# Tail of a hybrid decoder layer: SBUF regions placed at multiples of 256 bytes, and the output weights of the cross attention split two or three at a time

## The reference, cut to what matters

```
x = x + mixed @ w_out[l]
x = x + memory_cross_attention(rms_norm(x, ln_xattn[l]), mem_n, xa_wq[l], xa_wkv[l], xa_wo[l], xa_qn[l], xa_kn[l])
x = x + conv_glu_ffn(rms_norm(x, ln_ffn[l]), ffn_w_up[l], ffn_conv_w[l], ffn_conv_b[l], ffn_w_down[l])

def memory_cross_attention(h, mem_n, w_q, w_kv, w_o, q_norm, k_norm):
    q = rms_norm((h @ w_q).reshape(b, t, XA_HEADS, XA_HEAD_DIM), q_norm)
    k, v = jnp.split(mem_n @ w_kv, 2, axis=-1)
    logits = jnp.einsum('bthd,bmhd->bhtm', q, k).astype(jnp.float32) * XA_HEAD_DIM ** -0.5
    probs = jax.nn.softmax(logits, axis=-1).astype(v.dtype)
    o = jnp.einsum('bhtm,bmhd->bthd', probs, v).reshape(b, t, D_MODEL)
    return o @ w_o

def conv_glu_ffn(h, w_up, conv_w, conv_b, w_down):
    gate, val = jnp.split(h @ w_up, 2, axis=-1)
    gate = causal_depthwise_conv(gate, conv_w, conv_b)
    return (jax.nn.silu(gate) * val) @ w_down
```

## Time and profile before

| | |
|---|---|
| median of 3 runs | 1897.95 us (1896.48 to 1898.26) |
| the profiled execution, its time | 1897.06 us |
| the profiled execution, span from its first to its last instruction | 1895.3 us |
| TensorE busy, of the span | 1754.5 us (93%), 8076 matmuls |
| VectorE busy, of the span | 890.4 us (47%) |
| ScalarE busy, of the span | 677.4 us (36%) |
| mean granted clock of TensorE | 0.965 of full speed |
| moved by DMA | 121.32 MB, mean 64 GB/s |

### The profile page before, as it was taken

The page is one execution under the profiler, slowest core; times in us unless marked ns, Lnnn a source line. Parts: engine busy times, 40 slices in busy tenths (PEclk is TensorE's granted clock), DMA queues, the critical chain, the costliest instruction groups (busy, mean ns, idle before and its releaser), DMA issues.

```text
span 1895.3 us, 20863 instructions
## 1 busy us (share of the span) xinstructions
PE 1754.5 (93%) x8076; PEld 1378.8 (73%) x8076; DVE 890.4 (47%) x1487; ACT 677.4 (36%) x1218; POOL 74.2 (4%) x119
## 2 busy tenths in 40 slices
PE   6999998988888768799997999999999999999997
PEld 5787666555667545678886888888888888888886
DVE  4315584464545664645233424555543455555322
ACT  5224104543452353535333313434333333434221
POOL 2001430000001001000000000000000000000000
PEclk9999998898999889899998999999999999999999
DMA  4122000100011021430001203333322333333222
GB/s 136 45 46 45 23 1 12 34 3 9 12 34 56 22 88 35 171 119 23 1 1 45 73 1 94 96 94 95 89 73 95 102 110 91 121 92 103 84 95 95
DMA packets 166922, 121.32 MB, mean 64 GB/s; under 512 B 23448, under 2 KB 140456, under 8 KB 166824
## 3 DMA queue, kind: packets, MB, share of 16 engines
q1 hardware_dynamic: 165496, 115.53, 20.4%
q10 hardware_dynamic: 1328, 4.46, 0.6%
HBM read 115.77 MB, written 4.19 MB: 63 GB/s over the span
## 4 chain that ended last, share of the span: by engine, by line
PE 57%; DVE 1%; DMA 1%; ACT 0%; issue 0%; DVEq 0%
PE tail_b L101 18%; PE tail_b L99 17%; PE tail_b L100 17%; PE tail_b L2058 2%; PE tail_b L2033 1%; PE tail_b L2022 0%; PE tail_b L2045 0%; DMA tail_wr<-in_xa_wo 0%; PE tail_b L1970 0%; DVE tail_wl L1734 0%; DMA tail_wr<-in_w_out 0%; PE tail_b L2177 0%; PE tail_b L2093 0%; DVE tail_xs L1769 0%; ACT tail_xs L1569 0%
## 5 line engine op out<-in xcount | busy, mean ns | idle before, releaser
L1890 DVE TENSOR_TENSOR ff_wl<-ff_wr,ff_wh 128x512 fp32r<-128x512 f32 (+1 forms) x176 | 168.7, 959 | 345.9 <-ACT ff_wh L1677 345.9
L1677 ACT ACTIVATE ff_wh<-ff_wr 128x512 fp32r<-128x512 f32 (+1 forms) x176 | 148.7, 846 | 394.4 <-PE tail_b L101 394.4
L101 PE MATMUL tail_b<-HH,ff_wl 128*128 128x512 f32 x704 | 277.9, 395 | 0.0
L100 PE MATMUL tail_b<-HL,ff_wh 128*128 128x512 f32 x704 | 277.5, 394 | 0.0
L99 PE MATMUL tail_b<-HH,ff_wh 128*128 128x512 f32 x704 | 276.6, 393 | 0.0
L99 PE MATMUL mix_gb<-HH,mix_wh 128*128 128x512 f32 x432 | 178.5, 413 | 7.7 <-ACT slots L444 3.8
L100 PE MATMUL mix_gb<-HL,mix_wh 128*128 128x512 f32 x432 | 171.8, 398 | 0.0
L101 PE MATMUL mix_gb<-HH,mix_wl 128*128 128x512 f32 x432 | 171.6, 397 | 0.0
L99 PE MATMUL tail_b<-tail_wh,HH 128*128 128x512 f32 x384 | 154.8, 403 | 8.9 <-DVE tail_wl L1734 8.6
L100 PEld LDWEIGHTS tail_b<-HL,ff_wh 128*128 128x128 f32 x704 | 132.2, 188 | 31.6
L99 PEld LDWEIGHTS tail_b<-HH,ff_wh 128*128 128x128 f32 x704 | 132.2, 188 | 31.2
(11 more groups left out here) (311 smaller groups left out, 2672.0 us busy)
## 6 DMA issues: line engine op xcount, KB each, us to landing
ff_wr<-in_ffn_w_up SPq DMA_DIRECT2D x88, 512.0 KB, 3.9
ff_wr<-in_ffn_w_down SPq DMA_DIRECT2D x88, 256.0 KB, 2.8
mix_wr<-in_w_in SPq DMA_DIRECT2D x26, 512.0 KB, 3.6
mix_wr<-in_xa_wkv SPq DMA_DIRECT2D x16, 512.0 KB, 3.6
XR<-in_x SPq DMA_DIRECT2D x8, 512.0 KB, 6.2
tail_wr<-in_w_out SPq DMA_DIRECT2D x16, 256.0 KB, 5.4
XR<-in_x ACTq DMA_DIRECT2D x1, 4096.0 KB, 18.3
tail_wr<-in_xa_wq SPq DMA_DIRECT2D x16, 256.0 KB, 4.6
```

The lines of the kernel that those rows point to most:

```text
L100: pe.matmul(out, hi_w, lo_x, start=False, stop=False)
L101: return pe.matmul(out, lo_w, hi_x, start=False, stop=last)
L1677: act.activation(part(FWH[m % FPART], m), part(FWR[m % FRAW], m), ACT.Copy).then_inc(w_hi, 1)
L1890: dve.tensor_tensor(part(FWL[m % FPART], m), part(FWR[m % FRAW], m), part(FWH[m % FPART], m), ALU.subtract)\
```

## The change

It has three parts. First, the parts KEYS and HIGH of the region start at the next multiple of 256 bytes, and the region itself too. Second, the splits of the 16 pieces of xa_wo no longer stand in two groups of eight. A table `X_WEIGHTS` says which pieces are split in which step i, and at which of three places of the step: 0 is after the first query product's norm, 1 after the second's, 2 after the normalisation. Third, the first output product, `x_unit(0)`, moves on TensorE from the beginning of step 7 to behind the second query half of that step, and `x_add(0)` on VectorE accordingly.

```
-    LOW, KEYS, HIGH = R0, R0 + B * SLOT, R0 + (B + 4) * SLOT
+    line = lambda at: -(-at // 256) * 256
+    LOW, KEYS = R0, line(R0 + B * SLOT)
+    HIGH = line(max(KEYS + 16 * 1024, R0 + (B + 4) * SLOT))
...
+        X_WEIGHTS = {(NT - 2, 0): (WX, WX + 3), (NT - 2, 1): (WX + 3, WX + 6), (NT - 2, 2): (WX + 6, WX + KT),
+                     (NT - 1, 2): (WX + KT, WX + 11), (NT, 0): (WX + 11, WX + 14), (NT, 2): (WX + 14, WX + 2 * KT)}
...   on ScalarE, for i in range(1, NT + 1)
                 queries(i - 1)
+                for s in range(*X_WEIGHTS.get((i, 0), (0, 0))):
+                    hi(s)
                 if i < NT:
                     query_stats(i, 1)
-                if i == NT - 2:
-                    for s in range(WX, WX + KT):
-                        hi(s)
+                for s in range(*X_WEIGHTS.get((i, 1), (0, 0))):
+                    hi(s)
                 exps(i - 1)
-                if i == NT - 1:
-                    for s in range(WX + KT, WX + 2 * KT):
-                        hi(s)
+                for s in range(*X_WEIGHTS.get((i, 2), (0, 0))):
+                    hi(s)
...   on VectorE, for i in range(1, NT + 1)
                 if i + 1 < NT:
                     query_norm(i + 1, 0)
-                elif i == NT - 1:
-                    x_add(0)
-                else:
+                elif i == NT:
                     x_add(1)
+                for s in range(*X_WEIGHTS.get((i, 0), (0, 0))):
+                    lo(s)
                 if i < NT:
                     query_norm(i, 1)
                 else:
                     x_add(2)
-                if i == NT - 2:
-                    for s in range(WX, WX + KT):
-                        lo(s)
+                if i == NT - 1:
+                    x_add(0)
+                for s in range(*X_WEIGHTS.get((i, 1), (0, 0))):
+                    lo(s)
                 if i >= 2:
                     probabilities(i - 2)
                 maxima(i - 1)
                 normalise(i - 1)
-                if i == NT - 1:
-                    for s in range(WX + KT, WX + 2 * KT):
-                        lo(s)
+                for s in range(*X_WEIGHTS.get((i, 2), (0, 0))):
+                    lo(s)
...   on TensorE, for i in range(1, NT + 1)
                 if i + 1 < NT:
                     query(i + 1, 0)
-                elif i == NT - 1:
-                    x_unit(0)
-                else:
+                elif i == NT:
                     x_unit(1)
                 query_transposes(i - 1)
                 if i < NT:
                     query(i, 1)
                 else:
                     x_unit(2)
+                if i == NT - 1:
+                    x_unit(0)
...   in build
-            slots_at = -(-nc.sbuf_base // 32) * 32
+            slots_at = -(-nc.sbuf_base // 256) * 256
+            sb(attn, "to_line", [P, (slots_at - nc.sbuf_base) // 4]) if slots_at > nc.sbuf_base else None
```

## The result

The changed kernel takes 1868.68 us (median of 4 runs, 1866.8 to 1869.63) against 1898.11 us before (4 runs, 1896.48 to 1900.79). The ratio is 0.9842, with a 95% interval from 0.9825 to 0.9859. The profiled execution took 1867.99 us, 29.07 us less than that of before.

The account below looks back on a forecast made before the run. TensorE, busy 93% of the span, was taken as the bound. From 1897.06 us, 9.1 for the order and 19.2 for the placing left 1868.8; with the median 0.9 above, 1870 us, range 1865 to 1880.

Parts of the forecast that it names:

- The wait and its price: Attention step 6, value products waiting for the probability copies: the stall costs 11.6 us, of which 1.4 us stay.
- The new wait of step 8: First product with the second half of the output weights waits for the last two splits: 1.1 us.
- The loads: Step 6: slots four to six are full by about 1010 us, in time for the second three splits.
- rival D: Longer loads hold VectorE in step 6 again for some 9 us, while new addresses gain 19: 1879 us; chance 0.05.
- The claim on x_unit(0): In its old place, directly behind step 6's value products at about 1017 us, it would wait for the last two splits.
- The placing: Feed-forward and tail_wh1 products: an operand off a 256-byte line costs 5 to 6 ns per matmul; aligning gains 19.2 us.
- The comparison within the trace: Before the change, same instruction: 0.2269 us per matmul with tail_wh0, on a line; 0.2333 with tail_wh1, off one.
- Rival B: Feed-forward pace improves by half only, something beside the address holding it: 9.6 us less gain, 1880 us; chance 0.08.
- Rival C: New addresses do nothing and tail_wh1 is slow for another reason: 1889 us; chance 0.08.
- rival E: Feed-forward operands in equal places of a line collide, each matmul at 0.24 us: 1911 us; chance 0.03.
- The rule of two read ports: Weight load and moving operand have separate SBUF read ports; by it the new addresses gain 0, time 1889 us.
- The sum: Whole kernel: 1897.06 less 9.1 for the order and 19.2 for the addresses is 1868.8; forecast 1870 us.

Follow-up runs that it names:

- its own kernel: The changed kernel with x_unit(0) and x_add(0) back in their old places at the beginning of step 7: 1870.35 us, against 1868.73 us for the changed kernel beside it.
- the order alone: The changed kernel with KEYS and HIGH back at their old addresses, new order of splits and first output product kept: 1888.06 us, ratio 0.9949 to the kernel before.
- the placing alone: The kernel before with only KEYS and HIGH moved to multiples of 256 bytes, old order kept: 1879.09 us, ratio 0.9917.

## Why the prediction was right, point by point

**The wait and its price.** Right. The old stall cost 11.6 us, and step 6 has 21.27 - 19.69 = 1.6 us of it left, where 1.4 was predicted. The wait is 1.2 us and the products behind it take 0.1 us longer than undisturbed. The new wait of step 8 was predicted at 1.1 us and is 0.9. The order is then worth 11.6 - 1.6 - 0.9 = 9.1 us. That this is the predicted sum to the tenth is luck: the two remainders are off by 0.2 each, one up and one down. Measured by itself the order was worth 8.9 us in its stage and 9.9 in the medians.

**The loads.** Right: no wait for a load in front of the copies of step 6, and thus rival D (the wait only changes its place) is out. The claim on x_unit(0) is shown by its own kernel.

**The placing.** Right in sign, place and nearly in size. From the first to the last matmul of the feed-forward it was 738.23 us and is 721.82, so 16.4 us gained where 10.1 + 5.5 = 15.6 were predicted; the pace is 0.2267, the bound, and not 0.2270. The products with tail_wh1 were predicted to gain 3.6 us. From the first matmul of the tail (783.02 before, 782.37 after) to that of the feed-forward (1146.58 and 1133.93) 12.0 us are gained, and less 9.1 that leaves 2.9; the stages of the order alone and of the changed kernel differ by the same 2.9. A reason is to be seen: in the second half of the mixers' output product, where from its fourth group on four transposes stand behind each 12 matmuls, the mean of 166 times from start to start fell from 233.0 to 229.7 only, while undisturbed stretches reached 226.9. Here too two misses, 0.8 us too little and 0.7 too much, cancel in the sum of 19.2.

**What it was argued from.** The comparison within the trace was enough to find the effect, but the prediction laid the slow pace to the operand that is off a line. The runs show another rule with the same result for this change: the kernel with everything off by 128 bytes is as fast as the changed one. The forecast held because HH, HL and the region LOW lay on a line, so that to be on a line and to be at distance 0 came to the same; that part was luck. The trace of before had it already: the third buffer of the up products, 192 bytes off, was faster than the two at 128 (229.3 ns against 233.1), and the down products with both operands at 192 came back to the fast pace after three to ten matmuls, though on average, with the slow start, they took 228.9 ns. Here are the last nine of one row of twelve; its last seven starts span 1.36 us, 0.227 each:

```profile
1450.69 0.40 PE L99 MATMUL tail_b<-ff_wh,ff_ahb 128*128 128x512 f32 x1
...
1451.15 0.39 PE L101 MATMUL tail_b<-ff_wh,ff_ax 128*128 128x512 f32 x1
...
1452.51 0.39 PE L101 MATMUL tail_b<-ff_wh,ff_ax 128*128 128x512 f32 x1
```

Rival B counted the lower 0.2318 of the up stage as something beside the address that holds the pace; it was the mean of the two buffers at 233.1 and the one at 229.3. Rival C is out by the placing alone, and rival E (equal places collide) by the pace of 0.2267 in the up products.

**The rule of two read ports.** The Trainium skill, "TensorE: Matmul & The Clock Gate", Step-by-step, says that loading the next weights doesn't take read bandwidth from the running product. By that, no distance between the two operands should matter. The measurement decides otherwise for these fp32r products: 226.7 ns at distance 0, 233.3 at 128, with no instruction changed. That the two reads meet in one memory is the plainest account of a dependence on their distance, but it is argued, not shown; no run here takes the weight load away. That the same distance of 64 has two paces shows that more than the address takes part.

**The sum.** Of the 29.07 us between the profiled executions, 9.1 are the order, 16.4 the feed-forward and 2.9 the rest of the placing; the other 0.65 us came before the tail, where nothing changed. The time after the last matmul is the same 10.45 us.

## What to carry to other kernels

Where TensorE is full, look at the time from one start to the next, not at durations: the same instruction on two buffers at different paces is an experiment that is already made. Place the moving and the stationary operands of fp32r products at the same address modulo 256, here worth 1% of the whole kernel for a few bytes of padding. Put elementwise work that another engine doesn't wait for yet behind what it does wait for, in portions that fit the idle time and the loads in flight; count each portion ahead of a needed copy at its full length less the slack.

## What was not expected of the hardware

- The pace of fp32r matmuls of 512 columns with a weight load each depends on the difference of the operands' addresses modulo 256: 226.7 ns at 0, 229 or 233 at 64, and in the products of the table 233 to 234 at 32, 96, 128, 160, 192 and 224. Why 64 can be better than its neighbours, and what chooses between its two paces, stays open.
- Matmuls that follow a group of four transposes keep a slower pace for about ten more, at distance 0 too (229.7 ns on average with the transposes in between, 226.9 without). Transposes aren't needed for that: in the kernel before, a row of 12 down products at distance 0 (from 1441.63 us on) stands right behind one at distance 192, and its paces are 228, 229, 234, 236, 224, 230, 236, 229, 232 and 231 ns before it is back at 226 to 227.
